# In the Strassen jobs of a SwiGLU block, the older job's product M3 is issued ahead of the newer job's M6

## The chip, the cores and the metric

The kernel runs on one core of a Trainium2 chip. The metric is the device time of one launch in microseconds; less is better.

## The reference: what is computed

Two layers with the weights of each layer given; every layer works on 512 prompt tokens and on 8 streams of 16 new tokens, 640 rows of 1024 in all:

```python
x = half_swiglu(x, ffn1_norm, ffn1_up, ffn1_down)   # x + 0.5 * (silu(a) * b) @ w_down, [a | b] = rms_norm(x) @ w_up
h = rms_norm(x, mix_norm)
q, k, v, qi, ki, wi, cb, cc, cx, gates = split_cols(h @ w_in)
# sparse attention over the top-k keys, a gated short convolution, both projected and gated
x = x + (g_a * y_a + g_b * y_b) @ w_out
x = half_swiglu(x, ffn2_norm, ffn2_up, ffn2_down)
```

and a last rms_norm. The width is 1024, the hidden width of a SwiGLU block 2816. Everything is float32. The change touches only the four SwiGLU blocks (two in each of two layers) and the additions to x at the end of each product with w_out or w_down.

## The kernel before, in words

Activations lie transposed: model width on partitions, the T = 640 tokens along the free axis, in two halves of HALF = 320. Each float32 operand is split into a high and a low part (`hi`, made by ScalarE, and `lo`, the rest, made by VectorE or by GpSimd for some weights), and a product is the sum of three matmuls, hi*hi, hi*lo and lo*hi.

A SwiGLU block begins with 2 * PLAIN = 6 plain tiles (three hidden blocks, their a and b halves). The rest is cut into NJ = 31 **jobs**. Each is one 2x2 Strassen-Winograd step with seven products M1 to M7: an "up" job makes one hidden block out of a 4-block-deep sum (12 matmuls of 320 columns per product), a "down" job adds a group of six hidden blocks into two rows of x (9 matmuls per product). The list is four up jobs (k = 0 to 3), four down (4 to 7), six up (8 to 13), four down (14 to 17), six up (18 to 23), four down (24 to 27) and three up (28 to 30). So each block has three places where a down job follows an up job: job 4, job 14 and job 24. The last four hidden blocks are multiplied by w_down in eight plain tiles of LAST = 4 blocks each, the **closing** tiles.

The order of everything is written out by hand, one program per engine, with counting semaphores between them:

- TensorE (`product` L888, `jobs`): for job k it issues M1(k), M4(k-1), M6(k), M3(k-1), M2(k), M7(k), M5(k). Products of one job accumulate on each other in PSUM: M5 then M3 in `right`, M1 then M2 in `left`, M6, M7, M4 in `middle`. Between two of them an engine reads the half result. M3(k-1) waits until VectorE has taken M5(k-1) out of `right`: for an up job that is `c22` (L1933, semaphore c22_out), for a down job `x_m5` (one of the L1959 rows, semaphore m5_added). M6(k) waits until ScalarE has copied M1 from `left` to `middle` (`m1_to_middle`, L1321). M7(k) waits for `keep_u_one` (L1339), M4(k) for `keep_u_two` (L1349).
- The weight of each product is a strip: M1 A11, M2 A12, M3 S4, M4 A22, M5 S1, M6 S2, M7 S3. The S strips are sums of blocks of the raw weights, made by VectorE (`add_strips`, L1908). Each has one home for its high and low part, so ScalarE's `hi_strip` (L1309) of the next job waits for the end of the product that still reads it: hi S2 of job k+1 for M6(k), hi S4 of job k for M3(k-1). VectorE's `lo_strip` (L1918) follows, or GpSimd's `low_strip` (L643) for A11, A12 and A22 from job 4 on.
- VectorE in the loop for job k: take M5(k-1) (`c22` or `x_m5`), lo S1(k), the sums of job k+1, lo S2(k+1), sum S4(k+1), take M3(k-1) (`c12` L1940 or `x_m3`), lo S4(k), the gates (L1946, L1953) or the additions to x, then the hidden block: three sums (`add_second_half`, L2011 to L2014) after every second half of a pair, their low parts (`lo_g_sums`, L2031, 1280 columns, which waits for ScalarE's `keep_g_sums` L1391), lo S3(k+1), the low part of the gated block.
- The first matmuls of a down group need the sums of the whole group (g_sums_ready) and its pairs (g_ready).
- A closing tile c-loop (`passes`, L723) runs over the four last hidden blocks; in the first tile the last two blocks each have a wait for g_ready. On VectorE `closing` adds a tile to x (L1869), and `norm_block` then makes the low part of the next input (L1822) and adds the squares for the next norm (L1833), waiting for ScalarE's h_hi and sq of that row. `first_linear` of the next stage starts with the rows in order and puts the sum over the squares (L773) ahead of its sixth block.

## Time and profile before

| | us |
|---|---|
| median of 3 runs | 2685.0 (2684.85 to 2686.2) |
| the profiled execution | 2684.13 |
| its span, first to last instruction | 2682.3 |
| TensorE matmul busy in it | 2646.5 |
| VectorE busy | 2031.9 |
| ScalarE busy | 1347.6 |
| GpSimd busy | 916.8 |

The granted TensorE clock has a mean of 0.998 of full speed over the span. The four SwiGLU blocks repeat each other: their job loops lie at about 67 to 407, 972 to 1312, 1395 to 1735 and 2300 to 2640 us. Rows below are mostly from the last one. In the rows, "lin" and "bank" are the PSUM tensors in which `left`, `middle` and `right` lie; [x <- y] behind a row is the idle time of its engine before it and who ended it.

### The profile page before, as it was taken

To read this page: it belongs to the slowest core of one execution; us is meant where nothing else is said; L and a number is where in the kernel's file an instruction comes from. 1 tells how busy PE (TensorE), PEld (TensorE's weight loads), DVE (VectorE), ACT (ScalarE), POOL (GpSimd) and SP (SyncE) were. 2 spreads that over 40 slices of the span, in tenths; PEclk is the share of its full clock that TensorE was granted. 3 is DMA by queue.
4 is the path that set the end of the run, shared out by engine and by line. 5 is a ranking of instruction groups with operands and counts; after the bars stand their busy time and mean duration, and the time that the engine had idled before them with its cause. 6 is when DMAs were issued, how large, how long until landed. Compare 5 with 4: busy or idle time off the path is not lost. (4 is left out here: it accounts for less than half of the span.)

```text
span 2682.3 us, 48363 instructions
## 1 busy us (share of the span) xinstructions
PE 2646.5 (99%) x18372; PEld 2583.1 (96%) x18372; DVE 2031.9 (76%) x3489; ACT 1347.6 (50%) x2498; POOL 916.8 (34%) x642
## 2 busy tenths in 40 slices
PE   9999999999999999999999999999999999999997
PEld 8999999998999999999999999999989999999997
DVE  8998976887433699989689889668773347989885
ACT  5555555536322355555555555464463233555553
POOL 1243333355433203343302433333544332043431
PEclk9999999999999999999999999999999999999999
DMA  3222223233122222222222222223332222222222
GB/s 133 81 93 84 82 73 101 90 124 125 60 78 86 73 75 89 79 95 79 79 79 79 87 87 79 77 91 97 134 103 72 74 91 63 82 93 79 91 83 71
DMA packets 89785, 234.28 MB, mean 87 GB/s; under 512 B 8817, under 2 KB 42353, under 8 KB 89073
## 3 DMA queue, kind: packets, MB, share of 16 engines
q1 hardware_dynamic: 74784, 204.11, 23.0%
q10 hardware_dynamic: 14800, 27.51, 3.0%
q8 instruction: 125, 2.05, 0.3%
q14 instruction: 76, 0.61, 0.1%
HBM read 223.32 MB, written 8.27 MB: 86 GB/s over the span
## 5 line engine op out<-in xcount | busy, mean ns | idle before, releaser
L589 POOL TENSOR_TENSOR w_lo<-w_raw,w_hi 128x1024 fp32r<-128x1024 f32 (+1 forms) x178 | 365.8, 2055 | 627.5 <-ACT w_hi L1253 612.5
L643 POOL TENSOR_TENSOR lo_A<-raw_even,hi_A 128x512 fp32r<-128x512 f32 (+1 forms) x168 | 229.8, 1368 | 646.7 <-ACT hi_A L1309 645.6
L1253 ACT ACTIVATE w_hi<-w_raw 128x1024 fp32r<-128x1024 f32 (+1 forms) x174 | 168.7, 970 | 475.8 <-PE lin L723 346.8
L723 PE MATMUL lin<-h_hi,w_hi 128*128 128x320 f32 x1600 | 374.1, 315 | 5.3 <-DVE tmp L1809 2.7
L723 PE MATMUL lin<-h_hi,w_lo 128*128 128x320 f32 x1600 | 364.5, 309 | 0.0
L723 PE MATMUL lin<-h_lo,w_hi 128*128 128x320 f32 x1600 | 364.2, 309 | 0.0
L643 POOL TENSOR_TENSOR lo_A<-raw_odd,hi_A 128x512 fp32r<-128x512 f32 (+1 forms) x156 | 234.6, 1504 | 369.7 <-ACT hi_A L1309 369.4
L723 PEld LDWEIGHTS lin<-h_hi,w_hi 128*128 128x128 f32 x1600 | 264.9, 188 | 19.2 <-issue 14.6
L723 PEld LDWEIGHTS lin<-h_lo,w_hi 128*128 128x128 f32 x1600 | 267.5, 188 | 0.0
L723 PEld LDWEIGHTS lin<-h_hi,w_lo 128*128 128x128 f32 x1600 | 267.3, 188 | 0.0
L888 PE MATMUL bank<-h_hi,hi_A 128*128 128x320 f32 x704 | 217.6, 309 | 0.0
L888 PE MATMUL bank<-h_hi,lo_A 128*128 128x320 f32 x704 | 217.5, 309 | 0.0
L888 PE MATMUL bank<-h_lo,hi_A 128*128 128x320 f32 x704 | 217.5, 309 | 0.0
L1309 ACT ACTIVATE hi_S<-lin 128x512 fp32r<-128x512 f32 (+1 forms) x240 | 130.2, 553 | 121.3 <-DVE lin L1908 59.0
L1918 DVE TENSOR_TENSOR lo_S<-lin,hi_S 128x512 fp32r<-128x512 f32 (+1 forms) x240 | 150.5, 628 | 15.2 <-ACT hi_S L1309 13.5
L888 PE MATMUL bank<-T_hi,lo_S 128*128 128x320 f32 x480 | 148.3, 309 | 0.0
L888 PE MATMUL bank<-T_hi,hi_S 128*128 128x320 f32 x480 | 148.3, 309 | 0.0
L888 PE MATMUL bank<-T_lo,hi_S 128*128 128x320 f32 x480 | 148.3, 309 | 0.0
L1309 ACT ACTIVATE hi_A<-raw_even 128x512 fp32r<-128x512 f32 (+1 forms) x192 | 112.9, 588 | 59.7 <-PE lin L888 36.1
L1309 ACT ACTIVATE hi_A<-raw_odd 128x512 fp32r<-128x512 f32 (+1 forms) x180 | 105.3, 585 | 63.2 <-PE bank L888 62.4
L888 PE MATMUL lin<-T_hi,lo_S 128*128 128x320 f32 x432 | 133.5, 309 | 0.0
L888 PE MATMUL lin<-T_hi,hi_S 128*128 128x320 f32 x432 | 133.5, 309 | 0.0
(420 smaller groups left out, 7778.5 us busy)
## 6 DMA issues: line engine op xcount, KB each, us to landing
w_raw<-wts SPq DMA_DIRECT2D x144, 512.0 KB, 3.5
raw_even<-wts SPq DMA_DIRECT2D x80, 512.0 KB, 4.3
raw_odd<-wts SPq DMA_DIRECT2D x72, 512.0 KB, 4.2
raw_even<-wts SPq DMA_DIRECT2D x48, 384.0 KB, 3.7
raw_odd<-wts SPq DMA_DIRECT2D x48, 384.0 KB, 3.7
w_raw<-wts SPq DMA_DIRECT2D x32, 256.0 KB, 2.6
caches<-kcache_in ACTq DMA_DIRECT2D x16, 512.0 KB, 4.2
caches<-vcache_in ACTq DMA_DIRECT2D x16, 512.0 KB, 4.9
```

The source lines that it names most:

```text
L589: ins = nc.gpsimd.tensor_tensor(w_lo[:, s, cols], w_raw[:, s, cols], w_hi[:, s, cols].bitcast(F), ALU.subtract)
L643: nc.gpsimd.tensor_tensor(strip_lo[name][:, cols], raw_pair[k % 2][:, block_, cols], strip_hi[name][:, cols].bitcast(F), ALU.subtract).the ...
L723: ins = nc.tensor.matmul(out[:, half, :], w, a[:, half * HALF:(half + 1) * HALF], start=first and n == 0, stop=last and n == 2)
L888: ins = nc.tensor.matmul(out, w[i][:, c * P:(c + 1) * P], a[j], start=opens and c == n == 0, stop=c == blocks - 1 and n == 2, skip_group_c ...
L1253: nc.scalar.activation(w_hi[:, s, 0:cols], w_raw[:, s, 0:cols], ACT.Copy).then_inc(hi_ready.sem, 1)
L1309: nc.scalar.activation(strip_hi[name][:, cols], src, ACT.Copy).then_inc(strip_hi_done[name].sem, 1)
L1918: nc.vector.tensor_tensor(strip_lo[name][:, cols], src, strip_hi[name][:, cols].bitcast(F), ALU.subtract).then_inc(strip_ready[name].sem, 1)
```

## The change

Four edits. (1) On TensorE, from job 4 on, M3(k-1) is issued ahead of M6(k); before, and for jobs 2 and 3 still, M6(k) goes first. (2) At the first down job (FIRST_DOWN = 4): ScalarE makes `m1_to_middle` of job 4 at the end of the loop of job 3, ahead of `keep_g_sums` and the strips S3 and S1 of job 4, instead of behind them; VectorE takes M5(3) (`c22`) in the loop of job 3 ahead of the two `lo_g_sums`, instead of at the head of job 4. (3) In the first pair of closing tiles TensorE issues the blocks as tile 0: 0, 1, 2; tile 1: 0; tile 0: 3; tile 1: 1, 2, 3, so that one block of tile 1 stands between the third and the last of tile 0; the loop over the other three pairs keeps its order. (4) In `closing`, which also serves the product with w_out, VectorE adds row j+1 to x ahead of `norm_block` of row j; only for the last row of the whole kernel the old order stays.

```diff
@@ -44,7 +44,7 @@
 
 
 PLAIN = 3
-DVE_JOBS = 4
+DVE_JOBS = FIRST_DOWN = 4
 SPLIT_GROUPS = 3
 HIDDEN = list(range(6)) + [6 * g + i for g in range(1, SPLIT_GROUPS) for i in (0, 3, 1, 4, 2, 5)] + list(range(6 * SPLIT_GROUPS, FB))
 JOBS = [("up", p) for p in range(PLAIN, 7)] + [("down", d) for d in range(KB // 2)]
@@ -973,8 +973,12 @@
                 for k in range(2, NJ):
                     m1(L, q + k)
                     m4(L, q + k - 1)
-                    m6(L, q + k)
-                    m3(L, q + k - 1)
+                    if k >= FIRST_DOWN:
+                        m3(L, q + k - 1)
+                        m6(L, q + k)
+                    else:
+                        m6(L, q + k)
+                        m3(L, q + k - 1)
                     m2(L, q + k)
                     m7(L, q + k)
                     m5(L, q + k)
@@ -993,15 +997,22 @@
                     linear(L, n0 + k, m0 + k, k % 2, h_hi, h_lo, frees_rows=k == 2 * PLAIN - 1)
                 n0, m0 = n0 + 2 * PLAIN, m0 + 2 * PLAIN
                 jobs(L, f, q, m0)
-                with pe.Fori(0, KB // 2) as i:
-
-                    pe.wait_ge(g_ready.sem, g_ready.count(L, f * FB + FB - 2))
+                for s, c in [(0, c) for c in range(LAST - 1)] + [(1, 0), (0, LAST - 1)] + [(1, c) for c in range(1, LAST)]:
+                    if c == 0:
+                        pe.wait_ge(evacuated.sem, evacuated.count(L, m0 + s - 1))
+                        pe.wait_ge(lo_ready.sem, lo_ready.count(L, n0 + s + 1))
+                    if s == 0:
+                        pe.wait_ge(g_ready.sem, g_ready.count(L, f * FB + LAST_AT + c + 1))
+                    ins = passes(res(s), s, c, last_hi[c], last_lo[c], c == 0, c == LAST - 1)
+                    if c == LAST - 1:
+                        ins.then_inc(tile_done.sem, 1)
+                n0, m0 = n0 + 2, m0 + 2
+                with pe.Fori(0, KB // 2 - 1) as i:
+
                     for s in range(2):
                         pe.wait_ge(evacuated.sem, evacuated.count(L, m0 + s - 1 + 2 * i))
                         pe.wait_ge(lo_ready.sem, lo_ready.count(L, n0 + s + 1 + 2 * i))
                         for c in range(LAST):
-                            if s == 0 and c >= LAST - 2:
-                                pe.wait_ge(g_ready.sem, g_ready.count(L, f * FB + LAST_AT + c + 1))
                             ins = passes(res(s), s, c, last_hi[c], last_lo[c], c == 0, c == LAST - 1)
                         ins.then_inc(tile_done.sem, 1)
 
@@ -1451,7 +1462,7 @@
                 first_job(L, f, q, n, m)
                 for k in range(2, NJ):
                     more = k + 1 < NJ
-                    if k > 2:
+                    if k > 2 and k != FIRST_DOWN:
                         m1_to_middle(L, q + k, m)
                     if more:
                         hi_strip(L, q + k + 1, "A11", "M1")
@@ -1472,6 +1483,8 @@
                     keep_u_two(L, q + k)
                     if is_up(k - 1) and not waiting(k - 1):
                         keep_g(L, q + k - 1)
+                    if k + 1 == FIRST_DOWN:
+                        m1_to_middle(L, q + k + 1, m)
                     if is_up(k) and not is_up(k - 1):
                         keep_waiting(L, q + k - 1 - KB // 2)
                     if second_half(k - 1) and more and not is_up(k + 1):
@@ -1857,7 +1870,8 @@
             def closing(L, n0, m0, p, factor, next_q=None):
                 arm(3 * L + p)
                 dve.wait_ge(armed.sem, armed.count(L, p))
-                for j in range(KB):
+
+                def add_row(j):
                     dve.wait_ge(tile_done.sem, tile_done.count(L, n0 + j + 1))
                     if (L, p, j) == (DEPTH - 1, 3, KB - 1):
                         for half, signal in enumerate((half_left, evacuated.sem)):
@@ -1869,7 +1883,14 @@
                         nc.vector.scalar_tensor_tensor(out=halves(x[:, j, :]), in0=res((m0 + j) % 2), scalar=factor,
                                                        in1=halves(x[:, j, :]), op0=ALU.mult,
                                                        op1=ALU.add).then_inc(evacuated.sem, 1)
+                add_row(0)
+                for j in range(KB):
+                    last = (L, p, j) == (DEPTH - 1, 3, KB - 2)
+                    if j + 1 < KB and not last:
+                        add_row(j + 1)
                     norm_block(L, p, j)
+                    if last:
+                        add_row(j + 1)
                     if next_q and j == KB - 5:
                         add_strips(*next_q, "S1")
                         add_strips(*next_q, "S2")
@@ -2128,11 +2149,12 @@
                 for k in range(2, NJ):
                     more = k + 1 < NJ
                     opens_next = second_half(k - 1) and more and not is_up(k + 1)
-                    if k != 3:
+                    if k not in (3, FIRST_DOWN):
                         if is_up(k - 1):
                             c22(L, q + k - 1)
                         else:
                             x_m5(L, q + k - 1)
+                    if k != 3:
                         lo_strip(L, q + k, "S1")
                     if k + 1 < DVE_JOBS:
                         lo_strip(L, q + k + 1, "A11")
@@ -2165,6 +2187,8 @@
                         lo_strip(L, q + 3, "S1")
                     if second_half(k - 1):
                         add_second_half(L, q + k - 1)
+                    if k + 1 == FIRST_DOWN:
+                        c22(L, q + k)
                     if second_half(k - 2) and is_up(k):
                         lo_g_sums(L, q + k - 2)
                     if opens_next and k == 3:
```

## Rows read from the trace of the kernel before

**Rows 1.** The page: its first line and the engines' busy time.

```profile
span 2682.3 us, 48363 instructions
...
PE 2646.5 (99%) x18372; PEld 2583.1 (96%) x18372; DVE 2031.9 (76%) x3489; ACT 1347.6 (50%) x2498; POOL 916.8 (34%) x642
```

**Rows 2.** Waits of TensorE in total: waiter <- releaser: us, times, longest.

```profile
PE lin L888 <- DVE tmp L1933: 4.9, 4, 1.2
...
PE bank L888 <- ACT bank L1321: 3.9, 4, 1.0
...
PE lin L723 <- DVE g_lo L2046: 2.8, 4, 0.7
...
PE lin L723 <- issue: 2.1, 3, 1.8
```

**Rows 3.** Chain of waits, last block: start, us, matmuls of one product.

```profile
2426.35 1.76 PE lin L888 x12
...
2461.99 1.32 PE lin L888 x9
```

**Rows 4.** Timeline of TensorE: first matmul of jobs 4, 5 and 6.

```profile
2335.45 0.31 PE L888 MATMUL bank<-b_hi,hi_A 128*128 128x320 f32 x1
...
2348.29 0.31 PE L888 MATMUL bank<-b_hi,hi_A 128*128 128x320 f32 x1
...
2357.53 0.31 PE L888 MATMUL bank<-b_hi,hi_A 128*128 128x320 f32 x1
```

**Rows 5.** Timeline at job 4: M3(3), VectorE, ScalarE's u2(4), M5(4) taken.

```profile
2342.46 0.41 PE L888 MATMUL lin<-h_hi,hi_S 128*128 128x320 f32 x1 [1.22 <-DVE tmp L1933]
...
2337.08 2.91 DVE L2031 TENSOR_TENSOR g_sums_lo<-g_sums,g_sums_hi 128x1280 fp32r<-128x1280 f32 x2
...
2341.93 0.48 DVE L1933 TENSOR_TENSOR tmp<-lin,tmp 128x320 f32<-128x320 f32 x1
...
2347.62 0.42 ACT L1349 ACTIVATE tmp<-bank 128x320 f32<-128x320 f32 x1
...
2349.78 0.49 DVE L1959 SCALAR_TENSOR_TENSOR x<-bank,x 128x320 f32<-128x320 f32 x1
```

**Rows 6.** Timeline at job 14: M3(13), ScalarE, VectorE.

```profile
2453.46 0.31 PE L888 MATMUL lin<-h_hi,hi_S 128*128 128x320 f32 x1
...
2442.56 0.49 ACT L1309 ACTIVATE hi_S<-lin 128x384 fp32r<-128x384 f32 x1
...
2448.46 1.26 ACT L1391 ACTIVATE g_sums_hi<-g_sums 128x1280 fp32r<-128x1280 f32 x1
...
2443.07 0.56 DVE L1918 TENSOR_TENSOR lo_S<-lin,hi_S 128x384 fp32r<-128x384 f32 x1 [0.19 <-ACT hi_S L1309]
...
2447.77 0.48 DVE L2014 TENSOR_TENSOR g_sums<-tmp,g_sums 128x320 f32<-128x320 f32 x1
...
2451.64 0.48 DVE L1933 TENSOR_TENSOR tmp<-lin,tmp 128x320 f32<-128x320 f32 x1
```

**Rows 7.** Timeline at jobs 10 and 11: GpSimd, VectorE, M3(10).

```profile
2409.49 2.59 POOL L643 TENSOR_TENSOR lo_A<-raw_odd,hi_A 128x512 fp32r<-128x512 f32 x1 [3.63 <-ACT hi_A L1309]
...
2409.44 1.48 DVE L2031 TENSOR_TENSOR g_sums_lo<-g_sums,g_sums_hi 128x1280 fp32r<-128x1280 f32 x1
...
2412.25 0.69 DVE L1918 TENSOR_TENSOR lo_S<-raw_odd,hi_S 128x512 fp32r<-128x512 f32 x1 [1.32 <-ACT hi_S L1309]
...
2413.66 0.48 DVE L1933 TENSOR_TENSOR tmp<-bank,tmp 128x320 f32<-128x320 f32 x1
...
2417.38 0.31 PE L888 MATMUL bank<-h_hi,hi_S 128*128 128x320 f32 x1
```

**Rows 8.** Timeline at closings: low weight tiles, last square sum.

```profile
2633.97 1.42 POOL L589 TENSOR_TENSOR w_lo<-w_raw,w_hi 128x512 fp32r<-128x512 f32 x1 [1.91 <-ACT w_hi L1253]
...
1337.43 2.90 POOL L589 TENSOR_TENSOR w_lo<-w_raw,w_hi 128x1024 fp32r<-128x1024 f32 x1 [2.61 <-ACT w_hi L1253]
...
920.53 0.82 DVE L1833 TENSOR_TENSOR acc<-acc,sq 128x640 f32<-128x640 f32 x1
```

## The prediction

> **What bounds the kernel now.** I read the page first: TensorE is busy for 2646.5 of 2682.3 us [rows 1]. No other engine is near that, so only what stands between two matmuls can be won or lost. The list of TensorE's waits says how much there is to win: four waits of 1.2 us for `c22` (L1933), four of 1.0 us for `m1_to_middle` (L1321), four of 0.7 us for the low part of the last hidden block (L2046), and three "issue" waits, the longest 1.8 us [rows 2]. Each first kind comes once per SwiGLU block, so the two job waits sit at one place of the block. The chain of waits, read in order of time, gives TensorE's price list: an up product takes 1.76 us (12 matmuls, 0.147 us each), a down product 1.32 us [rows 3]. Last the timelines: how long before its use on TensorE each half result is ready. The four blocks repeat each other to some 0.02 us, so one block is worked out and multiplied by four.
>
> **Job 4, the place of the waits.** From M1(4) to M1(5) TensorE needs 12.84 us [rows 4]. The products in between are five of a down job and two of an up job, M4(3) and M3(3): 5 x 1.32 + 2 x 1.76 = 10.12 us. So 2.72 us are lost: the two waits and a slow first matmul after each, about 0.1 us a time. The change takes away both. M3(3) would start after M1(4) and M4(3), at 2335.45 + 1.32 + 1.76 = 2338.53. VectorE can do `c22` of job 3 where now `lo_g_sums` starts, at 2337.08, so it is ready at 2337.56. The copy of M1(4), which ScalarE makes earlier, has till 2340.29.
>
> What is late next is VectorE. It has hardly an idle moment from 2337 till it takes M5(4) at 2349.78, ready at 2350.27 [rows 5]; the edit reorders its work there and removes none. In the old order M3(4) did not need M5(4) taken before 2352.25. In the new one it stands ahead of M6(5), and TensorE is 2.72 us earlier: it would come at 2352.25 - 2.72 - 1.32 = 2348.21. It must wait till about 2350.32 (0.05 us from the end of an instruction to its waiter, as at 2342.41 and 2342.46 [rows 5]). M4(4), one product ahead, waits too, for ScalarE's u2(4) at 2348.04 [rows 5]; the two waits overlap. From M3(4) it is five down products and one slow start to M1(6): 2350.32 + 6.6 + 0.1 = 2357.03, against 2357.53 now [rows 4]. So of 2.72 us 0.5 stay. If VectorE loses 0.7 us more to GpSimd there, since `c22`, which reads PSUM, no longer stands between two instructions that both engines want the port for, the head costs 0.2. I take -0.3 each, -1.2 for four; bounds: -2.7 each (VectorE's chain shrinks with the waits) and +0.3.
>
> **Jobs 14 and 24, where there is no wait now.** These heads get the new order of TensorE but none of the edits that prepare job 4. M3(13) starts at 2453.46 and `c22` of job 13 ends at 2451.64 + 0.48 = 2452.12 [rows 6]: 1.34 us to spare. Two things eat it. First, M3(13) moves ahead of M6(14), a down product: 1.32 us earlier. Second, the same swap one job before moves M6(13) behind M3(12), an up product: 1.76 us later. ScalarE's hi S2(14) waits for M6(13) (its home is what M6(13) reads), and VectorE's lo S2(14) waited for that hi S2 already (0.19 us idle before 2443.07 [rows 6]). From there VectorE goes on without a stop worth naming to `c22` of job 13: sum S4, `c12`, lo S4, the gates, three sums, the low pair, `lo_g_sums`, lo S3. One hold-up gives way: ScalarE's copy of the group sums starts at 2448.46, 0.21 us after the last sum ended at 2448.25 [rows 6], held by the copy before it; behind a later sum it would start after 0.03, so 0.18 us are absorbed. `c22` comes 1.76 - 0.18 = 1.58 us later against TensorE's order, M3(13) finds it 1.34 - 1.32 - 1.58 - 0.05 = -1.61, and with the slow first matmul each such head loses 1.7 us. There are two per block, eight in all: +13.8. Behind it, at M3(14), about 0.5 us remain to spare, so nothing is added and nothing is given back. Bounds: 0 (if the chain has slack that the rows do not show) and 2.4 each, if one more GpSimd instruction of 0.7 us falls into the chain.
>
> **The other jobs.** Down behind down: M5 is taken some 2.7 us before M3 starts, less 1.32 leaves 1.4; nothing. Up behind up: M3(10) starts at 2417.38, M5(10) is taken at 2414.14: 3.24 us [rows 7], less 1.76 leaves 1.48. The later hi S2 holds VectorE by about 1.6 us; after a job with `lo_g_sums` 1.32 us of idle time ahead of lo S3(11) takes that up [rows 7], after the other kind the hold-up comes through as about 1.3 of 1.64. Both end 0.2 to 1.2 us above zero by this count. Here one more thing can go: at 2409.44 VectorE's 1.48 us low part starts 0.05 us ahead of GpSimd's low strip, which then lasts 2.59 us instead of its usual 1.3 [rows 7]: the one that is second waits for the first. In the new order ScalarE hands GpSimd its strip about 0.3 us earlier relative to VectorE, so GpSimd would go first and VectorE loses 1.3 us. Then M3 of such jobs stands at about -0.05. I take 0.1 us for each of 16 such places, +1.6; bounds 0 and 1.2 each.
>
> The Trainium skill (SBUF — State Buffer, "SBUF: two separate sides") has this as a lock: a VectorE instruction with two SBUF inputs and a GpSimd instruction that reads SBUF exclude each other, and whichever starts first keeps the port pair for its whole length. This case's trace agrees, the 2.59 us row being its second one. It speaks against the change in so far as a shift of some tenths can turn the order round and cost a whole GpSimd instruction; what it would cost here is the third rival.
>
> M7(k) now waits for u1 with one product between instead of two: ScalarE needs 0.5 us after M6 and has 1.32 or 1.76; nothing. The DMA queue's loads of job k+2 follow the low strips A22 and S3, of which A22 hangs on M4(k-1), whose place is the same; nothing.
>
> **The closings.** At the first closing tile TensorE waits 0.7 us for the last hidden block, 0.86 with the slow start [rows 2]. A block is six matmuls, 0.88 us, so the one put in between covers it, if tile 1's low weights are there: GpSimd made them at 2633.97 to 2635.39 [rows 8], 4.6 us ahead. -0.86 x 4 = -3.4; bounds -3.4 and 0 (tile 1 must not wait for something else).
>
> VectorE's row j+1 ahead of `norm_block` j: in most closings it had time before. At the one between the layers, where it also makes strips, it was late, and TensorE waited 1.8 us as "issue" (in truth for GpSimd's low tile, 1337.43 to 1340.33 [rows 8], itself started late behind ScalarE and VectorE). I take -1.3 there; bounds 0 and -2.4. After w_out tiles are 7 us apart, and the new order does row 6's norm only after tile 7: three more instructions of 0.7 to 0.8 us ahead of the last sum of squares, which now ends at 921.35 [rows 8], about 0.9 us before TensorE wants it. Part is spent waiting for ScalarE now, so about 1.1 us come on top: +0.3 at two places, +0.6; bounds 0 and +1.2.
>
> **Sum.** -1.2 + 13.8 + 1.6 - 3.4 - 1.3 + 0.6 = +10.1 us on the profiled execution's 2684.1: 2694.2. The median shown is 0.9 above that execution, so 2695.1. I forecast 2695 us, 0.4% slower.
>
> **The rivals.**
> *The late heads don't wait (ends faster).* The place is VectorE's chain from lo S2(14) to `c22`; the price is my +13.8, and it decides whether that chain really hangs on the end of M6(13). For it: 0.19 us of waiting at its head is a thin sign, and earlier work of VectorE now gets 1.76 us more room. Against: it is order of issue, and everything in the chain is serial. Time: 2695.1 - 13.8 - 1.6 = 2679.7 with heads at -0.5, 2679. If VectorE also lets job 4 keep all of its 2.72 us: 2670. Chance 0.12.
> *Half of it.* The chain shrinks by a few tenths each (GpSimd's strip falls beside instructions that read PSUM), heads at 0.8 us: 2695.1 - 7.2 = 2688, or less with no loss in the steady jobs, 2686. Chance 0.14; it lies around the bound.
> *The lock turns round everywhere.* GpSimd goes first in every up job, and M3 waits 0.6 us at 16 places: +8 more, 2703. Chance 0.12. For it: 0.05 us between the two starts. Against: time that VectorE loses ahead of hi S2 is time that it would have waited.
> *As worked out.* Chance 0.62, its own range 2690 to 2701.
>
> **How the numbers follow.** 2684 to 2703 leaves out the first rival and a little of the third. Less than 0.2% (5.4 us, about what a measurement of this kernel can tell from no change) is 2679.6 to 2690.4: the second rival but for its upper end, a little of the forecast. So faster 0.11, same 0.14, slower 0.75.
>
> **What would show it.** Right: in the waits of TensorE the four for L1321 are gone, the ones for L1933 have not gone but turned into about eight of 1.5 us, at the heads of jobs 14 and 24; at job 5 a new wait for an L1959 row or for u2 (L1349) of 1 to 2 us; no wait for L2046. M1(6) still at about 22.1 us behind M1(4) less 0.5 (now 22.08 [rows 4]). Wrong: no wait at job 14, with `c22` ending before M4(13) does; job 4 to 6 shorter by over 1.5 us; or waits in the middle of up jobs that add up to more than the heads.

## The result, and the profile after

The changed kernel takes 2705.1 us (median of 4 runs, 2704.82 to 2705.71), the kernel before 2684.93 beside it (2684.38 to 2686.2): ratio 1.0074, 95% interval 1.0061 to 1.0086. It is slower by 0.74%, twice what was forecast (+10.1 us), and 2.1 us above the range's upper end. The sign and the largest term were right; two terms were not.

The page, and the waits of TensorE in total (us, times, longest), of the changed kernel:

```profile
span 2703.3 us, 48331 instructions
...
PE 2656.7 (98%) x18372; PEld 2584.6 (96%) x18372; DVE 2051.8 (76%) x3489; ACT 1328.3 (49%) x2498; POOL 902.6 (33%) x642
```

```profile
PE lin L888 <- DVE tmp L1954: 10.1, 8, 1.3
PE bank L888 <- DVE x L1980: 4.6, 16, 0.7
...
PE bank L888 <- ACT tmp L1360: 2.7, 4, 0.7
PE lin L723 <- issue: 2.6, 1, 2.6
PE lin L723 <- DVE x L1883: 2.4, 2, 1.2
...
PE bank L773 <- DVE acc L1846: 1.2, 3, 0.9
...
PE lin L723 <- POOL w_lo L589: 0.5, 1, 0.5
```

Against [rows 2]: the four waits for `m1_to_middle` are gone, and so are the four for the last hidden block (L2046). The four for `c22` (now L1954) became eight of 1.27 us. The row to look at next is the second. Sixteen waits for an addition to x: four of 0.65 us at job 5, and twelve of 0.17 us that no row of before has. The last four rows belong to the closings; their waits were 1.8 and 0.6 us in two places before.

The total of such a view doesn't say what a wait costs, since a wait can take the place of another and is followed by a slow matmul. So the table below gives lengths of jobs: from the first matmul of M1(k) to that of M1(k+1), less the same in the kernel before, in us, mean of the four blocks. They agree to 0.06, but for jobs 4 and 5 of e1 and e9, which vary by the clock, and job 4 of e3, where the mean is 1.28 in the first block and nothing in the others. "Down group" is the sum over jobs 6 to 8 or 16 to 18, "late head" is job 14 or 24; where nothing stands the difference is under 0.05. Two smaller differences are left out: +0.02 to 0.05 at jobs 11, 13, 21 and 23 with the new order, and about +0.16 at jobs 15 and 25 of e6 and e7. "Loops" is the sum over the four job loops, "rest" what is outside them; in the changed kernel, e3, e5, e7, e8, e9 and e12 the rest holds one stretch of 3.4 us (6.8 in e8) at half the granted clock that the kernel before has not. Where such a stretch lies between the layers (e3, e5, e7, e8, e9) it costs 0.9 us, and 1.9 in e8, by comparison with kernels that are alike there and have no such stretch.

| kernel | job 4 | job 5 | late head | down group | loops | rest |
|---|---|---|---|---|---|---|
| changed | -2.06 | +1.96 | +1.53 | +0.59 | +19.5 | +1.6 |
| e1 | +3.3 | | +1.53 | +0.57 | +32.9 | 0 |
| e2 | | | | | 0 | +4.1 |
| e3 | +0.3 | | | | +1.3 | -1.9 |
| e4 | -2.05 | +1.61 | | +0.10 | -1.3 | -3.5 |
| e5 | -2.07 | +1.60 | +0.13 | +0.10 | -0.4 | +0.8 |
| e6 | -2.06 | +1.96 | +0.28 | +0.59 | +10.7 | +0.4 |
| e7 | | | +0.28 | +0.59 | +10.5 | +1.1 |
| e8 | -2.07 | +1.96 | +1.53 | | +12.3 | +3.0 |
| e9 | +2.7 | +0.12 | +0.29 | | +13.6 | -2.5 |
| e10 | -2.06 | +0.10 | | | -7.8 | -3.2 |
| e11 | -2.06 | +0.68 | | +0.10 | -5.1 | -3.5 |
| e12 | -2.07 | +1.14 | +0.29 | | -1.5 | -2.2 |

(In e4, e5 and e11 the 0.10 is in the first group alone, at job 6.)

**The late head.** Timeline of the changed kernel at job 14, which answers to [rows 6]: M3(13), ScalarE's hi S2(14) (two in one row), VectorE from lo S2(14) to `c22` of job 13; columns are start, us, and in brackets the idle time before and who ended it.

```profile
2471.17 0.42 PE L888 MATMUL lin<-h_hi,hi_S 128*128 128x320 f32 x1 [1.27 <-DVE tmp L1954]
...
2461.91 0.98 ACT L1320 ACTIVATE hi_S<-lin 128x384 fp32r<-128x384 f32 x2
...
2462.43 0.56 DVE L1939 TENSOR_TENSOR lo_S<-lin,hi_S 128x384 fp32r<-128x384 f32 x1 [0.93 <-ACT hi_S L1320]
...
2468.75 1.49 DVE L2052 TENSOR_TENSOR g_sums_lo<-g_sums,g_sums_hi 128x1280 fp32r<-128x1280 f32 x1 [0.61 <-ACT g_sums_hi L1402]
...
2470.63 0.48 DVE L1954 TENSOR_TENSOR tmp<-lin,tmp 128x320 f32<-128x320 f32 x1
```

VectorE idles 0.93 us for hi S2(14) where it idled 0.19. From the start of lo S2 to that of `c22` it needs 2470.63 - 2462.43 = 8.20 us, against 8.57 before.

**Down behind down.** Timeline of the changed kernel at the head of job 8: VectorE, with the row of job 7's u1 and the pair of rows (x2) that takes c21(6) and c11(6), and TensorE's last matmul of job 7 and first two of M1(8).

```profile
2389.81 0.49 DVE L1980 SCALAR_TENSOR_TENSOR x<-tmp,x 128x320 f32<-128x320 f32 x1 [1.08 <-ACT tmp L1350]
2390.30 0.69 DVE L1939 TENSOR_TENSOR lo_S<-lin,hi_S 128x512 fp32r<-128x512 f32 x1
2391.03 0.69 DVE L1929 TENSOR_TENSOR lin<-raw_even,lin 128x512 f32<-128x512 f32 x1
2391.64 0.48 DVE L1980 SCALAR_TENSOR_TENSOR x<-bank,x 128x320 f32<-128x320 f32 x1
2392.04 0.55 DVE L1939 TENSOR_TENSOR lo_S<-lin,hi_S 128x384 fp32r<-128x384 f32 x1
2392.50 0.88 DVE L1980 SCALAR_TENSOR_TENSOR x<-bank,x 128x320 f32<-128x320 f32 x2
...
2392.96 0.31 PE L888 MATMUL lin<-g_sums_hi,lo_S 128*128 128x320 f32 x1
2393.43 0.42 PE L888 MATMUL bank<-h_hi,hi_A 128*128 128x320 f32 x1 [0.17 <-DVE x L1980]
2393.69 0.32 PE L888 MATMUL bank<-h_lo,hi_A 128*128 128x320 f32 x1
```

M1(8) writes `left`, in which M2(6) left its result. It is free only when `x_c11` of job 6 has been taken, 2392.50 + 0.88 = 2393.38. That addition needs nothing but M2(6), done a whole job earlier; it stands behind u1(7), lo S2(8), sum S4(8), `x_m3`, lo S4 and `x_c21`, and u1(7) waits 1.08 us for ScalarE, which waits for M6(7). The wait is 0.17 us, but job 7 is 0.40 longer: from the matmul ahead of the wait to the first of M1(8) it is 0.47 us and from there to the next 0.26, where a step without a wait is 0.15. In the kernel before, the same pair of rows ended at 2374.98 + 0.88 = 2375.86 and M1(8) began at 2376.01, so only 0.15 us lay between them, of which a waiter takes 0.05 (2393.38 to 2393.43 in the rows above): 0.10 us were to spare.

**A closing.** Timeline of the changed kernel at the last tiles of the first block: a low weight tile on GpSimd, with VectorE's acc beside it; ScalarE's sq waits for VectorE's acc, the high weight tile stands behind it, GpSimd's low tile behind that, and TensorE's first matmul of the next product last.

```profile
432.97 1.47 POOL L589 TENSOR_TENSOR w_lo<-w_raw,w_hi 128x512 fp32r<-128x512 f32 x1 [2.05 <-ACT w_hi L1264]
...
433.19 1.93 DVE L1846 TENSOR_TENSOR acc<-acc,sq 128x640 f32<-128x640 f32 x1
...
435.15 0.74 ACT L1278 ACTIVATE sq<-x 128x640 f32<-128x640 f32 x1 [1.54 <-DVE acc L1846]
435.80 1.04 ACT L1264 ACTIVATE w_hi<-w_raw 128x1024 fp32r<-128x1024 f32 x1
...
436.92 2.85 POOL L589 TENSOR_TENSOR w_lo<-w_raw,w_hi 128x1024 fp32r<-128x1024 f32 x1 [2.49 <-ACT w_hi L1264]
...
439.87 0.38 PE L723 MATMUL lin<-h_hi,w_hi 128*128 128x320 f32 x1 [1.21 <-DVE x L1883]
```

The bracket of the last row names VectorE's row addition, but that ended at 439.52; the low tile ended at 436.92 + 2.85 = 439.77, 0.10 us ahead of the matmul. In the kernel before the same tile ended 433.74 and the matmul began 433.84, with 0.17 us of idle time.

### The profile page after: what moved, and what is told of

It reads as the page before. It is cut to its first block and busy times, and to the rows that moved or that the text cites. A ratio compares the mean times of both kernels' runs of the same rounds, so it can differ in the third digit from the quotient of the medians.

```text
span 2703.3 us, 48331 instructions
## 1 busy us (share of the span) xinstructions
PE 2656.7 (98%) x18372; PEld 2584.6 (96%) x18372; DVE 2051.8 (76%) x3489; ACT 1328.3 (49%) x2498; POOL 902.6 (33%) x642
## 5 line engine op out<-in xcount | busy, mean ns | idle before, releaser
L589 POOL TENSOR_TENSOR w_lo<-w_raw,w_hi 128x1024 fp32r<-128x1024 f32 (+1 forms) x178 | 372.4, 2093 | 622.5 <-ACT w_hi L1264 606.6
L643 POOL TENSOR_TENSOR lo_A<-raw_odd,hi_A 128x512 fp32r<-128x512 f32 (+1 forms) x156 | 212.1, 1360 | 387.7 <-ACT hi_A L1320 386.3
L1320 ACT ACTIVATE hi_S<-lin 128x512 fp32r<-128x512 f32 (+1 forms) x240 | 120.5, 555 | 48.1 <-DVE lin L1929 48.1
L888 PEld LDWEIGHTS bank<-h_hi,hi_A 128*128 128x128 f32 x704 | 132.1, 188 | 5.2 <-DVE x L1980 5.2
L888 PE MATMUL lin<-T_lo,hi_S 128*128 128x320 f32 x432 | 133.5, 309 | 0.0
```

The costliest lines, as they stand in the source:

```text
L589: ins = nc.gpsimd.tensor_tensor(w_lo[:, s, cols], w_raw[:, s, cols], w_hi[:, s, cols].bitcast(F), ALU.subtract)
L643: nc.gpsimd.tensor_tensor(strip_lo[name][:, cols], raw_pair[k % 2][:, block_, cols], strip_hi[name][:, cols].bitcast(F), ALU.subtract).the ...
L888: ins = nc.tensor.matmul(out, w[i][:, c * P:(c + 1) * P], a[j], start=opens and c == n == 0, stop=c == blocks - 1 and n == 2, skip_group_c ...
L1320: nc.scalar.activation(strip_hi[name][:, cols], src, ACT.Copy).then_inc(strip_hi_done[name].sem, 1)
```

## The experiments

Twelve kernels. e5 to e8 were executed once each and have no interval; there the lengths of the jobs carry the argument, and the times only have to fit them. "New order" means M3(k-1) ahead of M6(k) on TensorE; edits 1 to 4 are numbered as in the section on the change.

**e1, the swap alone.** Edit 1, none of the others.

> The kernel before with edit (1) alone: M3(k-1) ahead of M6(k) from job 4 on, nothing prepared at job 4, closings as before. My theory: what costs is the later place of M6(k). ScalarE's u1(k) and hi S2(k+1) wait for it, and everything behind them in VectorE's queue comes late; TensorE then waits for c22 at M3(13) and M3(23) (1.5 us each, as in the changed kernel) and for x_c11(k-2) at M1(k) in jobs 6 to 8, 16 to 18 and 26 to 28 (0.6 us per group). Per block: head of job 4 +1.3 (M3(3) waits for the unprepared c22, 2342.46 in the old trace, and M6(4) now stands behind it), late heads +3.1, down groups +1.8, rest +0.1: 6.3, in all +25 us, 2710. Rival 'preparation is worth nothing': the job loops cost what they cost in the changed kernel, +19.5, 2704.5. Rival 'the closings made the loss': under +10, 2695 or less.

Measured 2716.73 us (ratio 1.0117, interval 1.0101 to 1.0132). The late heads and down groups cost here what they cost in the changed kernel. The time is 6.7 us above what was expected. The miss is at job 4, which costs 2.7 to 3.8 us a block and not 1.3: M3(3) waits 3.76 us in one piece, and the clock falls. Windows of its trace at that place (columns: us, busy us of PE, PEld, DVE, ACT, POOL, granted clock, DMA share, GB/s):

```profile
2358.00:2365.00 7.00, 4.89 (x34) 4.63 (x32) 6.97 (x10) 5.18 (x10) 1.95 (x2) 1.00 0.06 22
2366.00:2372.00 6.00, 5.35 (x20) 5.36 (x21) 3.04 (x6) 0.00 (x0) 1.04 (x1) 0.50 0.42 132
2373.00:2380.00 7.00, 7.00 (x50) 7.00 (x49) 6.42 (x12) 4.52 (x12) 2.37 (x3) 1.00 0.00 0
```

**e2, the rows' order alone.** Edit 4.

> The kernel before with edit (4) alone: VectorE adds row j+1 to x ahead of the norm of row j. Theory: this edit costs, since ScalarE's square of row j waits for VectorE's sum of row j-1, which now stands behind the addition of row j; the high part of tile j+2 stands behind that square on ScalarE and its low part behind it on GpSimd, and the first tile of the next stage starts late: +1.2 at each of the two ends of a first SwiGLU block, +1.5 to 2 between the layers, +0.3 at each end of a product with w_out: +5 us, 2690. Rival: the new order of the first two closing tiles delays the weights, and this edit alone costs nothing or gains at the end of layer 1: 2683 to 2685.

Measured 2691.55 us (1.0023, 1.0013 to 1.0032); its profiled execution, 2688.24, has a span 4.1 us longer than before's. The five stretches outside the loops changed by +0.34, +1.25, +1.73, +1.13 and -0.35 us. Its waits of TensorE:

```profile
PE lin L723 <- issue: 2.6, 1, 2.6
PE lin L723 <- DVE x L1870: 2.4, 2, 1.2
...
PE bank L773 <- DVE acc L1833: 1.2, 3, 0.9
```

The totals, counts and longest waits are those of the changed kernel's rows, so these waits are this edit's. The profiled execution was the quickest of ten: the other nine took 2690.1 to 2692.3 us, so by the medians the edit costs some 6 us. What the 2 us more are was not profiled.

**e3, the closing tiles alone.** Edit 3.

> The kernel before with edit (3) alone: one block of closing tile 1 between the last two blocks of tile 0. Theory: takes away four waits of 0.86 us and nothing else changes: -3.4 us, 2681.5. Rival: tile 0 ends 0.9 us later and the low weights of the tiles behind come late: no gain, 2684 to 2687.

Measured 2683.01 us (0.9991, 0.9982 to 1.0001). By the times alone this is not clear of no change. In the trace the four waits for L2046 are gone and three closings gain 0.83, 0.93 and 0.85 us. In the profiled execution the fourth gain is hidden, and 1.3 us are lost at job 4 of the first block, by two stretches of 3.4 us at half the granted clock (from 1341.8 and 109.6 us) that the kernel before has not.

**e4, M3 first at job 4 alone, prepared, and the closing tiles.** Edits 2 and 3, and edit 1 as

```diff
-                    if k >= FIRST_DOWN:
+                    if k == FIRST_DOWN:
                         m3(L, q + k - 1)
                         m6(L, q + k)
```

> Edits (2) and (3), and (1) only at job 4: M3(3) ahead of M6(4), everywhere else the old order; VectorE's closing order as before. Theory: no waits at jobs 14 and 24 and none for x_c11; at the head job 4 gets 2.06 us shorter as in the changed kernel, and job 5 loses about 0.8 (M4(4) waits for u2(4); M3(4) at its old place no longer waits for x_m5(4)) instead of 1.96: -1.25 per block, -5.0, and -3.4 at the closings: 2676.5. Rival 'VectorE has too much work at the first head whatever the order': the head gives 0.1 as in the changed kernel: 2681.

Measured 2679.3 us (0.998, 0.9971 to 0.9989), faster than the kernel before and than e3, and 2.8 us above what was expected. The head wins 2.05 us at job 4 and gives 1.71 back at jobs 5 and 6, where 0.8 was expected. M4(4) waits 0.69 us for u2(4), as named; not named was M1(6), which waits 0.40 us for `x_c11` of job 4.

**e5, M3 first at the three heads only.** As e4 with `k in (4, 14, 24)` and without edit 3.

> M3(k-1) ahead of M6(k) only at jobs 4, 14 and 24 (the first job behind another kind), with the edits that prepare job 4; closings as before. Theory (what the late heads pay is the swap one job EARLIER, at jobs 13 and 23, which moves M6(13) 1.76 us behind and with it hi S2(14), lo S2(14) and the chain to c22(13); the swap at job 14 itself eats only 1.32 of 1.34 us to spare): jobs 14 and 24 lose 0 to 0.1 us each, down behind down loses nothing (12 groups of 0.59 gone), job 4 to 6 as in the run of the first head alone, -0.33 a block. Loops about -1 us in all, profile 2683, time 2684. Rival (the swap at the head itself is what costs): +1.5 at each of eight places, 2695 us.

Measured 2684.49 us, span 2682.7. The same eight heads have the swap and lose 0.13 us each instead of 1.53.

**e6, M3 first from job 4 on but not at jobs 14 and 24**, with edit 2 and the closings as before:

> M3(k-1) ahead of M6(k) from job 4 on, but not at jobs 14 and 24, where the old order stands; job 4 prepared; closings as before. Theory: c22(13) is still 1.58 us late (M6(13) behind M3(12)), against 1.34 - 0.05 us to spare with M3(13) back behind M6(14): the late heads lose 0.3 to 0.5 us each instead of 1.53, and down behind down still loses 0.5 to 0.6 at 12 places. 8 x 0.4 + 12 x 0.59 - 1.3 + 0.6 = +9.6: 2694 us. Rival (the swap at the head itself costs): late heads 0, 2690 us or less.

Measured 2695.17 us. The old order at jobs 14 and 24 doesn't save them: 0.28 there and 0.16 at the next job, and the down groups still lose 0.59.

**e7, TensorE's order untouched, only ScalarE held.** In the kernel before, at `keep_u_one`:

```diff
+                if k >= 4:
+                    act.wait_ge(product_done["M3"].sem, product_done["M3"].count(L, q))
                 if k:
                     act.wait_ge(product_done["M6"].sem, product_done["M6"].count(L, q + 1))
```

> The kernel before with TensorE's order untouched; ScalarE alone is held: from job 4 on its copy u1(k) and the hi S2(k+1) wait for M3(k-1) too, 1.32 or 1.76 us later than M6(k). Theory (the lateness of what hangs on M6 is the whole cost, not the place of M3): late heads lose 0.3 to 0.5 us at 8 places (c22(13) 1.58 us late, 1.29 to spare, old place of M3), down behind down 0.5 to 0.6 at 12 places, job 4 something below 1. In all +8 to +13, 2693 to 2698 us. Rival (the place of M3 in TensorE's queue costs, VectorE takes a later S2 in its stride): within 2 us of before, 2686.

Measured 2695.76 us. Late heads 0.28, next jobs 0.16, down groups 0.59, to 0.01 us the figures of e6. Its timeline at the head of job 8, with TensorE's old order:

```profile
2382.21 0.49 DVE L1961 SCALAR_TENSOR_TENSOR x<-tmp,x 128x320 f32<-128x320 f32 x1 [1.08 <-ACT tmp L1341]
...
2384.90 0.87 DVE L1961 SCALAR_TENSOR_TENSOR x<-bank,x 128x320 f32<-128x320 f32 x2
...
2385.83 0.42 PE L888 MATMUL bank<-h_hi,hi_A 128*128 128x320 f32 x1 [0.17 <-DVE x L1961]
```

The idle 1.08 us and the wait of 0.17 are those of the changed kernel. So the down groups' loss comes from the time at which ScalarE takes M6 and needs no swap at all.

At the late head the number came about as expected (0.28, expected 0.3 to 0.5), but not by the wait that was expected. Timeline of e7 there: the copy of M1(14) (`m1_to_middle`), the first matmul of M6(14), `c22` of job 13, the first matmul of M3(13).

```profile
2461.76 0.42 ACT L1321 ACTIVATE bank<-bank 128x320 f32<-128x320 f32 x1
...
2462.23 0.41 PE L888 MATMUL bank<-g_sums_hi,hi_S 128*128 128x320 f32 x1
...
2462.94 0.48 DVE L1935 TENSOR_TENSOR tmp<-lin,tmp 128x320 f32<-128x320 f32 x1
...
2463.65 0.31 PE L888 MATMUL lin<-h_hi,hi_S 128*128 128x320 f32 x1
```

M1(14) starts at 2458.97, so M6(14) starts 3.26 us behind it where the two products ahead take 3.08; it begins 0.05 us after the end of the copy, and its second matmul comes 0.10 late. That is the 0.28. M3(13) finds `c22` done 0.23 us before it. The same holds in e6, in all eight late heads. In ScalarE's queue that copy stands behind the copy of the group sums, which waited 1.28 us for VectorE.

**e8, the changed kernel with `x_c11` straight behind `x_m5`.**

```diff
                             x_m5(L, q + k - 1)
+                            x_c11(L, q + k - 1)
 ...
                             x_c21(L, q + k - 1)
-                            x_c11(L, q + k - 1)
```

> The changed kernel with one move on VectorE: behind a down job, x_c11(k-1) stands straight behind x_m5(k-1) instead of behind x_m3, lo S4 and x_c21. Its product M2(k-1) is long done there. Theory (M1(k+1) waits for left to be free, because x_c11(k-1) stands in the queue behind u1 and S2, which hang on the later M6(k)): the twelve losses of 0.59 us down behind down go, -7 us; late heads unchanged at +1.53; first up job behind a down job the same or 0.2 later. 2698 us, the wait 'PE bank L888 <- DVE x L1980' of 4.6 us gone. Rival (another wait, sum S4 or c21, is 0.1 us behind it): 2702 us or more.

Measured 2699.44 us. Down groups 0, late heads unchanged, loops 7.1 us shorter than the changed kernel's. In the waits, sixteen have become the four at job 5:

```profile
PE lin L888 <- DVE tmp L1954: 10.1, 8, 1.3
...
PE bank L888 <- DVE x L1980: 2.6, 4, 0.7
```

**e9, every queue in TensorE's order.** Edits 1 to 3; from job 4 on ScalarE's hi S4(k) and silus(k-1) stand ahead of u1(k) and hi S2(k+1), and VectorE's work that hangs on M3(k-1), with c21 and c11, ahead of the work that hangs on M6(k); in outline:

```diff
+                    if k >= FIRST_DOWN:      # ScalarE
+                        hi_strip(L, q + k, "S4", "M3")
+                        if is_up(k - 1):
+                            silus(L, q + k - 1)
                     keep_u_one(L, q + k)
 ...
+                    if k >= FIRST_DOWN:      # VectorE
+                        of_m3()   # c12 or x_m3, lo S4, gates or x_c21, x_c11
+                        of_m6()   # x_u_one, lo S2, sum S4
```

> The changed kernel's order of TensorE everywhere from job 4 on, the closing tiles' edit, not the rows' order; and the queues of the other engines in the same order as TensorE's: on ScalarE hi S4(k) and the silus of k-1 ahead of u1(k) and hi S2(k+1), on VectorE c12/x_m3, lo S4, gates, c21 and c11 of k-1 ahead of u1(k), lo S2(k+1) and sum S4(k+1). Theory (M3 first costs only because the queues of ScalarE and VectorE still wait for the later M6 ahead of what M3 and M2 already allow; the work itself has room): the twelve down losses 0, late heads 0 to 0.3 instead of 1.53, head of job 4 at -0.3 to -0.5, tiles -0.86 x 4: 2679 to 2681 us. Rival (c22(13) needs lo S2 and sum S4 done ahead of it wherever they stand, and M6(13) itself is late): late heads still about 1.5, 2691 us.

Measured 2695.93 us (1.0043, 1.0028 to 1.0059). Late heads 0.29 and down groups 0, as the theory said, but job 4 lost 2.7 us where a gain was expected. Its timeline there:

```profile
2353.27 0.48 DVE L1959 TENSOR_TENSOR g_wait<-lin,tmp 128x320 f32<-128x320 f32 x1
...
2353.79 0.47 ACT L1370 ACTIVATE g_wait<-g_wait 128x320 f32<-128x320 f32 x1 [3.32 <-DVE g_wait L1959]
2354.16 0.42 ACT L1350 ACTIVATE tmp<-bank 128x320 f32<-128x320 f32 x1
...
2354.63 0.63 PE L888 MATMUL bank<-g_sums_hi,hi_S 128*128 128x320 f32 x1 [3.54 <-ACT tmp L1350]
```

M7(4) waits for u1(4), which now stands on ScalarE behind the silu of job 3, and that waits 3.32 us for `c12` on a VectorE that is far behind at this job. The edit repaired the late heads and the down groups and broke the head of job 4 by the same fault, a queue with an early and a late thing in the wrong order.

**e10, the tuned head.** e4, with `x_c11` as in e8, and on VectorE

```diff
+                    if k == FIRST_DOWN:
+                        c12(L, q + k - 1)
                     if not is_up(k):
                         x_u_one(L, q + k)
```

(and `c12` no longer at its old place behind them).

> The best run so far (M3 first at job 4 alone, job 4 prepared, closing tiles) with two moves on VectorE: c12(3) ahead of x_u1(4), lo S2(5) and sum S4(5) at job 4, and x_c11(k-1) straight behind x_m5(k-1). Theory (of the 2.06 us won at job 4, 1.6 go again at job 5 to two waits of order: M4(4) 0.69 for u2(4), which on ScalarE stands behind the silu that waits for c12(3), and M1(6) 0.40 for x_c11(4)): both waits shrink to 0 to 0.3, -0.5 to -1.2 a block, 2675 to 2677.5 us. Rival (VectorE is full of work from job 3 to job 5, so what is made earlier only puts the wait on x_m5(4)): within 1 us of the run before, 2679 us.

Measured 2673.04 us (0.9956, 0.9942 to 0.997), 2 us below the low end of what was expected: the fastest kernel of the study. Jobs 4 and 5 together are 1.96 us shorter a block. **e11, only the move of `c12`**:

> Of the two moves of the tuned head only one: c12(3) ahead of x_u1(4), lo S2(5) and sum S4(5) at job 4; x_c11(k-1) stays behind x_c21. Theory (M4(4)'s 0.69 us wait for u2(4) and its slow start of 0.16 come from the place of c12(3), M1(6)'s 0.40 us and its slow start from that of x_c11(4)): the first goes, the second stays or grows to 0.8, since nothing ahead of it takes time off TensorE now: jobs 4 and 5 together -1.2 to -1.5 us a block instead of -1.95, 2675 to 2677 us. Rival (c12 first alone lets VectorE run early enough for x_c11(4) too): -1.95, 2673 us.

Measured 2676.05 us (0.9967, 0.9955 to 0.998). So `c12` is worth 0.9 us a block and `x_c11` 0.7. What is left of the waits at this head in e11 is one of 0.42 us before M1(6), four times:

```profile
PE bank L888 <- DVE x L1972: 1.7, 4, 0.4
```

**e12, the new order everywhere, repaired.** e9 with the conditions at `k > FIRST_DOWN`, and at job 4 the head of e11.

> The changed kernel's order of TensorE on every job from 4 on, closing tiles, not the rows' order; the other queues in the same order from job 5 on, and at job 4 the tuned head (c12(3) alone ahead of u1(4); ScalarE's u1(4) and hi S2(5) ahead of the silus). Theory (the order of TensorE costs only by what the other queues make of it; the 3.5 us at job 4 of the run with all queues turned was the silu of job 3 standing ahead of u1(4) on ScalarE): no wait at job 4, 0.29 at each of the eight late heads, nothing down behind down: 2673 + 2.3 = 2675.5 us, range 2674.5 to 2677. Rival (the order itself costs, by waits that were masked at job 4): 2680 us or more.

Measured 2680.06 us (0.9981, 0.9971 to 0.9991), 3 us above the expected range's end and the rival's figure. Late heads and down groups are as expected, job 4 too. What was not expected is job 5, +1.14 against +0.10 in e10: M3(4), one product earlier, waits for M5(4) to be taken.

```profile
PE bank L888 <- DVE x L1978: 3.1, 4, 0.8
```

That is 4 us; 1 more is a stretch at half the clock near the start of the profiled execution.

## Why the prediction was wrong

The terms, forecast and measured, us over the four blocks. The first four are the changed kernel's own, from the lengths of its jobs; the closing tiles are e4's "rest", the rows' order is that of e2's profile.

| term | forecast | measured |
|---|---|---|
| head of job 4 (jobs 4 and 5) | -1.2 | -0.4 |
| late heads | +13.8 | +12.3 |
| down behind down | 0 | +7.0 |
| up behind up | +1.6 | +0.6 |
| closing tiles | -3.4 | -3.5 |
| rows' order in the closings | -0.7 | +4.1 |
| sum | +10.1 | +20.1 |

The two spans differ by 21.0. Of the 0.9 that is left 0.6 lies ahead of the first job loop. There the granted clock is 0.50 for 3.4 us from 9.4 us on (1.00 before), but e3, e6, e7 and e10 are 0.53 to 0.65 us longer at that place without such a stretch. It was not part of the sum, and its cause is not known.

**The step that failed** is "Down behind down: M5 is taken some 2.7 us before M3 starts, less 1.32 leaves 1.4; nothing." As far as it looked it was right: at jobs 6 to 8 no M3 waits. But the step looked only at the product that moved ahead and at what it waits for. The product that moved back, M6(k), has its own followers: u1(k) on ScalarE, then on VectorE u1(k), S2(k+1), sum S4(k+1) and all behind them. In the late heads this was followed through to `c22`; in the down jobs it was not followed to `x_c11`, on which M1 of the next job but one depends. e7 shows that the delay alone makes the loss, e8 that the place of `x_c11` does. The 0.10 us to spare stood in the trace of before, had the chain been followed to that row. This one term is 7.0 of the 10.9 us by which the 21.0 exceeds the forecast's 10.1.

**The rows' order** is the second step that failed, 4.8 us of the miss: it was forecast with the wrong sign. The step saw VectorE's x addition as late and let it go first. It left out that ScalarE's sq(j) waits for acc(j-1) and that the weight tile stands behind sq on ScalarE, with GpSimd's tile behind it: adding row j+1 first puts acc behind one more instruction. One more thing went against it, and it is a lock between two engines: acc takes 0.81 us at 425.76 in the kernel before and 1.93 in the row shown. GpSimd's low tile had started at 432.97 and lasted 1.47 us, to 434.44; acc, started at 433.19, ended 0.68 us after that. The Trainium skill (SBUF — State Buffer, "SBUF: two separate sides") gives this as a rule, the later of the two waits for the whole of the earlier one; this row agrees. It is no single case: of the 47 additions to acc 29 take 1.9 to 3.0 us in the changed kernel and in e2, where in the kernel before none takes more than 1.1. Each of the 29 starts while a low tile of GpSimd (L589) runs, and ends 0.68 or 0.69 us after it.

**Right, and the sizes.** *Late heads*: 1.53 us against 1.7 (eight times 1.7 is 13.6; the prediction's sum has 13.8). It takes both swaps, as the prediction had it: the head's without the earlier one costs 0.13 (e5), the earlier one without the head's 0.28 (e6), the delay of M6's followers without any swap 0.28 (e7), and both 1.53. That the prediction's terms also give 1.58 - (1.34 - 0.05) = 0.29 for e6 is luck: `c22` comes 1.39 us later there, which alone would cost 0.10, and what is waited for is the copy of M1(14), of which the prediction says nothing at this head. In the changed kernel the wait is the one that was worked out. M1(14) starts at 2466.66 and M3(13) at 2471.17, 4.51 us behind it and 1.43 later than the 3.08 us of the two products ahead; 1.61 was reckoned. Lo S2(14) starts 1.76 us later against M1(14), as reckoned (4.23 us ahead of it, 5.99 before), so what is missing is the chain on VectorE: 8.20 us where 8.57 less 0.18 was reckoned. *First head*: two waits at job 5, as named. Timeline of the changed kernel there, M4(4), M3(4) and VectorE's `x_m5`:

```profile
2365.54 0.42 PE L888 MATMUL bank<-g_sums_hi,hi_A 128*128 128x320 f32 x1 [0.68 <-ACT tmp L1360]
...
2367.78 0.41 PE L888 MATMUL bank<-g_hi,hi_S 128*128 128x320 f32 x1 [0.65 <-DVE x L1980]
...
2367.23 0.49 DVE L1980 SCALAR_TENSOR_TENSOR x<-bank,x 128x320 f32<-128x320 f32 x1
```

M1(4) starts at 2352.51, so M5(4) is taken 14.72 us behind it, against 2349.78 - 2335.45 = 14.33 before [rows 4, 5]: VectorE's chain was said not to grow and grew by 0.39 (why was not tried). Nor did job 4 get back all of its 2.72 us, but 2.06: M7(4) starts 0.10 us behind the end of VectorE's lo S3(4), which costs 0.45 us, and M1(5) 0.05 us behind the silu of job 3 on ScalarE (L1368) that frees `left`, which costs 0.19. The prediction asked of M7 only when u1 is ready. M1(6) starts 21.97 us behind M1(4) (mean of the blocks) against 22.08 before, 0.10 won a block and not the 0.5 of the count or the 0.3 taken. *Closing tiles*: 0.79 to 0.94 each (e4), 0.86 reckoned.

*The lock in the up jobs* turned as the third rival's premise had it, without its price. Timeline of the changed kernel at job 10, which answers to the first two of [rows 7]:

```profile
2428.43 1.44 POOL L643 TENSOR_TENSOR lo_A<-raw_odd,hi_A 128x512 fp32r<-128x512 f32 x1 [5.12 <-ACT hi_A L1320]
...
2428.63 2.59 DVE L2052 TENSOR_TENSOR g_sums_lo<-g_sums,g_sums_hi 128x1280 fp32r<-128x1280 f32 x1
```

GpSimd is first now and takes 1.44 us instead of 2.59, VectorE is second and takes 2.59 instead of 1.48. It lost 1.11 us, and no M3 waited: the up jobs lose 0.02 to 0.05 us each at a few places.

**Was the order itself bad?** Less than the changed kernel makes it look. With the queues of the other engines turned to match, the same order on TensorE costs 0.29 us at a late head, nothing in the down groups, and 1.04 us at job 5 against the old order there (e12 against e10). The only place where a kernel with the new order wins is job 4, 2.0 us a block with the two moves of e10, and the fastest kernel tried has the new order there alone. But that the order wins it is not shown: e1, with the order and without edit 2, loses 2.7 to 3.8 us at that place, and edit 2 with the old order was never run. Timeline of e10 at job 4: the copy of M1(4), `c22` of job 3, and the first matmul of M3(3).

```profile
2329.16 0.42 ACT L1332 ACTIVATE bank<-bank 128x320 f32<-128x320 f32 x1 [1.07 <-PE bank L888]
...
2329.27 0.48 DVE L1946 TENSOR_TENSOR tmp<-lin,tmp 128x320 f32<-128x320 f32 x1
...
2330.72 0.31 PE L888 MATMUL lin<-h_hi,hi_S 128*128 128x320 f32 x1
```

The copy that M6(4) needs is done at 2329.58 and `c22` at 2329.75, both 0.97 us or more ahead of the first product that could use them. So edit 2 alone might have taken both waits away with TensorE's order as it was.

## What to carry to other kernels

When two instructions of one queue change places, one goes forward and one goes back. Ask what the first waits for, and then, with the same care, everything that hangs on the second, through every other engine's queue, to the next instruction of the first engine that needs any of it; buffers come free there as well as data. A wait that is won at one place is only kept if the engines behind it had idle time; where they are in order of an older schedule, moving two ready instructions (`c12`, `x_c11`) ahead of waiting ones was worth 1.6 us a block here, where edits 1 and 2 at that head had brought 0.34 (e4).

## What the runs showed of the hardware

A wait costs TensorE some 0.26 us more than the idle time in its bracket, with the clock at full speed. In the kernel before, brackets of 0.97 and 1.22 us are all that stands at job 4, and 2.72 us are lost; at a late head of the changed kernel 1.27 goes with 1.53; at the head of job 8 0.17 goes with steps of 0.47 and 0.26 us where 0.15 is usual, 0.43 in all.

A long wait can cost the clock besides. Where TensorE waited 3.76 us (e1) or 3.54 us (e9) in one piece at job 4, the granted clock was 0.50 of full speed (1.2 GHz) for 3.4 or 6.8 us of the record, in all four blocks of both kernels. It fell before the wait ended in four of the eight (in the last block of e1 at 2365.5 us, where the wait ended at 2366.65) and 0.1 to 1.1 us after its end in the others. The waits in e1 grew by 3.76 - 1.22 - 0.97 = 1.57 us, job 4 by 2.7 to 3.8: the clock took the other 1.1 to 2.3.

Shorter waits had it now and then: the pair of 0.97 and 1.22 us at job 4 in one of sixteen cases (e3, first block; never in the kernel before, e2 and e7), the 1.8 us between the layers in four of eleven (e3, e5, e7 and e9; not in the kernel before, e1, e4, e6, e10, e11 or e12); the 2.6 us at the same place in e8 but not in the changed kernel or e2. No late head with its 1.27 us had it, in 24 cases (the changed kernel, e1 and e8). So a difference of 1 us outside the loops can be such a stretch, and one profile does not tell them apart; the lengths of the jobs do, which repeat from block to block to a few hundredths where the clock does not fall.
